# Two modulation panels among the sums of squares, and each down-projection panel split ahead of its tiles

## The reference, cut to what matters

```python
def rms_norm(x, w):
    return x * rsqrt(mean(x * x, axis=-1) + EPS) * w
c_act, cc_act = silu(c), silu(c_ctx)
mod  = split(c_act  @ w_mod[i] + b_mod[i], 6)      # sh1, sc1, g1, sh2, sc2, g2 for x
modc = split(cc_act @ w_mod[i] + b_mod[i], 6)      # the same for ctx
z  = (rms_norm(h,  norm1_w) * (1 + sc1)  + sh1)  @ w_in
zc = (rms_norm(hc, norm1_w) * (1 + csc1) + csh1) @ w_in
a = z[..., :384 + 256 + 32]                        # the "down" part: MLA queries, keys, rope
...                                                # attention mixers, FFN, second layer, second model
```

## Time and profile before

| what | us |
|---|---|
| median of 3 runs | 3116.35 (3114.63 to 3122.04) |
| the profiled execution | 3119.45, its span 3117.7 |
| PE busy in the span | 2812.8 (90%) |
| VectorE, ScalarE, GpSimd busy | 1359.5, 1217.7, 1117.6 |
| granted TensorE clock, mean | 0.951 of full speed |

### The profile page before, as it was taken

How to read it: one execution, slowest core, us unless ns; L and a number is a source line. 1 busy time by engine, 2 the same in 40 slices (tenths; PEclk the granted TensorE clock), 3 DMA queues, 4 the chain that set the end, 5 groups by cost and what they waited for, 6 DMA issues and landing times. The chain is left out here.

```text
span 3117.7 us, 52810 instructions
## 1 busy us (share of the span) xinstructions
PE 2812.8 (90%) x20541; PEld 2502.8 (80%) x20541; DVE 1359.5 (44%) x2405; ACT 1217.7 (39%) x1791; POOL 1117.6 (36%) x457
## 2 busy tenths in 40 slices
PE   6789879799889999888789899899889999988998
PEld 4557667588779999566679799899779989977898
DVE  2443533332343433444434543534564353456433
ACT  2322223333244444422345444444444444444443
POOL 0101020132235565111214455354425555632453
PEclk8899989899989999998999999999999999989999
DMA  5454034533336666211415566465225646622563
GB/s 173 131 180 147 14 83 127 156 91 104 94 109 192 188 194 191 83 29 41 88 48 152 164 197 189 141 198 165 95 82 162 188 138 197 190 84 68 149 186 97
DMA packets 570660, 413.54 MB, mean 133 GB/s; under 512 B 36566, under 2 KB 548252, under 8 KB 570524
## 3 DMA queue, kind: packets, MB, share of 16 engines
q1 hardware_dynamic: 570524, 411.69, 44.6%
HBM read 410.58 MB, written 2.88 MB: 133 GB/s over the span
## 5 line engine op out<-in xcount | busy, mean ns | idle before, releaser
L543 POOL TENSOR_TENSOR wlo<-raw,whi 128x768 fp32r<-128x768 f32 (+2 forms) x353 | 1020.3, 2894 | 1701.6 <-ACT whi L534 1701.2
L566 PE MATMUL psum<-xh_n,whi 128*128 128x256 f32 (+1 forms) x3208 | 932.3, 291 | 79.6 <-DVE rtmp L2612 21.7
L567 PE MATMUL psum<-xl_n,whi 128*128 128x256 f32 (+1 forms) x3208 | 915.1, 285 | 0.0
L568 PE MATMUL psum<-xh_n,wlo 128*128 128x256 f32 (+1 forms) x3208 | 914.7, 285 | 0.0
L543 DVE TENSOR_TENSOR wlo<-raw,whi 128x1280 fp32r<-128x1280 f32 (+2 forms) x353 | 531.2, 1505 | 665.3 <-ACT whi L534 665.1
L534 ACT ACTIVATE whi<-raw 128x2048 fp32r<-128x2048 f32 (+2 forms) x353 | 643.2, 1823 | 396.0 <-PE psum L925 171.8
L566 PEld LDWEIGHTS psum<-xh_n,whi 128*128 128x128 f32 x3208 | 615.4, 192 | 114.4 <-issue 57.7
L568 PEld LDWEIGHTS psum<-xh_n,wlo 128*128 128x128 f32 x3208 | 617.3, 192 | 5.5
L567 PEld LDWEIGHTS psum<-xl_n,whi 128*128 128x128 f32 x3208 | 616.4, 192 | 4.7
L923 PE MATMUL psum<-hidh,whi 128*128 128x256 f32 x1232 | 344.0, 279 | 7.0 <-issue 7.0
L925 PE MATMUL psum<-hidh,wlo 128*128 128x256 f32 x1232 | 343.6, 279 | 0.0
(11 more groups left out here) (337 smaller groups left out, 3804.3 us busy)
## 6 DMA issues: line engine op xcount, KB each, us to landing
raw<-in_ffn_w_in SPq DMA_DIRECT2D x176, 512.0 KB
raw<-in_w_in SPq DMA_DIRECT2D x136, 512.0 KB
raw<-in_w_ffn_in SPq DMA_DIRECT2D x132, 512.0 KB
raw<-in_w_mod SPq DMA_DIRECT2D x96, 512.0 KB
raw<-in_ffn_w_out SPq DMA_DIRECT2D x88, 512.0 KB
raw<-in_w_ffn_out SPq DMA_DIRECT2D x66, 512.0 KB
raw<-in_w_out SPq DMA_DIRECT2D x32, 512.0 KB
raw<-in_w_a_o SPq DMA_DIRECT2D x16, 256.0 KB
```

The costliest lines, as they stand in the source:

```text
L543: eng.tensor_tensor(wlo[slot][:, c0:c1], raw[raw_at[p0] % 3][:, c0:c1], whi[slot][:, c0:c1].bitcast(F32), ALU.subtract).then_inc(sem_, 1)
L566: pe.matmul(dst, sh, mh, start=start and n == 0, stop=False, skip_group_check=True)
L567: pe.matmul(dst, sh, ml, start=False, stop=False, skip_group_check=True)
L568: last = pe.matmul(dst, sl, mh, start=False, stop=n == len(pairs) - 1, skip_group_check=True)
```

## The change

On TensorE the first two modulation panels are taken out of the loop over pairs and put between the sums of squares, and the loop begins with the third panel. On VectorE the copies and vectors of these two panels go ahead of the reciprocal. On ScalarE the high part of down panel 0 goes ahead of the first `xh`, and that of panel j + 1 behind the `xh` tiles of pair j. On VectorE the low part of panel j goes ahead of the pair's `xl`. No arithmetic is added or left out. The line numbers of the changed kernel are 5 to 7 higher at the same instructions.

```diff
-        def pe_sum(pe, tag, nk, bk, cols):
-            for k in range(nk):
+        def pe_sum(pe, tag, nk, bk, cols, ks=None):
+            for k in ks or range(nk):
...
-            pe_sum(pe, ("norm1", 0), 8, 6, slice(0, T))
+            pe.wait_ge(*act_done.at("silu c"))
+            mod_rows(0)
+            pe_sum(pe, ("norm1", 0), 8, 6, slice(0, T), range(0, 2))
+            mod_sum(0)
+            mod_rows(1)
+            pe_sum(pe, ("norm1", 0), 8, 6, slice(0, T), range(2, 4))
+            mod_sum(1)
+            pe_sum(pe, ("norm1", 0), 8, 6, slice(0, T), range(4, 8))
...
-            pe.wait_ge(*act_done.at("silu c"))
-            for j in range(4):
+            pe.wait_ge(*dve_done.at("par"))
+            for j in range(1, 4):
                 mod_rows(2 * j)
-                if j == 1:
-                    pe.wait_ge(*dve_done.at("par"))
-                if j:
-                    open_panel(pe, j - 1)
-                    hi, lo = down_k(2 * j - 2)
-                    for g in range(6):
-                        down_tile(g, 2 * j - 2, hi, lo)
+                open_panel(pe, j - 1)
+                hi, lo = down_k(2 * j - 2)
+                for g in range(6):
+                    down_tile(g, 2 * j - 2, hi, lo)
                 mod_sum(2 * j)
                 mod_rows(2 * j + 1)
...
                 act_squares(act, tg, ...)
+                if l == 0:
+                    split_act(act, 0)
                 for k in range(8):
                     hi_of(k)
-                    if l == 0 and k % 2:
-                        split_act(act, k // 2)
+                    if l == 0 and k in (1, 3, 5):
+                        split_act(act, (k + 1) // 2)
...
-                dve_rstd(dve, tg, slice(0, T))
                 for j in range(4):
                     for m in (2 * j, 2 * j + 1):
                         mod_rows(m)
                         mod_vectors(m)
+                    if j == 0:
+                        dve_rstd(dve, tg, slice(0, T))
                     dve.wait_ge(*dve_done.at(("mod", "vectors", 2 * j + 1)))
                     factors(2 * j, 2 * j + 2)
                     scaled(2 * j)
                     scaled(2 * j + 1)
+                    split_dve(dve, j)
                     lo_of(2 * j)
                     lo_of(2 * j + 1)
-                    split_dve(dve, j)
```

More of the change, by code:

```diff
@@ L801, in down_tile @@
                 return pe.matmul(dst, lo[:, c0:c0 + n], xh[:, k, :], start=False, stop=k == 7, skip_group_check=True)
-            pe.wait_ge(*act_done.at("silu c"))
-            for j in range(4):
+            pe.wait_ge(*dve_done.at("par"))
+            for j in range(1, 4):
                 mod_rows(2 * j)
-                if j == 1:
-                    pe.wait_ge(*dve_done.at("par"))
-                if j:
-                    open_panel(pe, j - 1)
-                    hi, lo = down_k(2 * j - 2)
-                    for g in range(6):
-                        down_tile(g, 2 * j - 2, hi, lo)
+                open_panel(pe, j - 1)
+                hi, lo = down_k(2 * j - 2)
+                for g in range(6):
+                    down_tile(g, 2 * j - 2, hi, lo)
                 mod_sum(2 * j)
                 mod_rows(2 * j + 1)
[L814 to L818, removed]
+                hi, lo = down_k(2 * j - 1)
+                for g in range(6):
+                    m = down_tile(g, 2 * j - 1, hi, lo)
+                m.then_inc(panel_used, 1)
                 mod_sum(2 * j + 1)
```

## The result

Over all runs the changed kernel takes 3102.89 us (median of 16, 3087.58 to 3118.52) against 3117.94 for the one before (16 runs, 3108.44 to 3126.30). The ratio is 0.9948, 95% interval 0.9930 to 0.9967, so it is 15 us faster (10 to 22 by the interval). Forecast were 3103 and 13.2 us. The comparison of the two traces is therefore made at marks in the program and not at the end.

A forecast was written before the change was run, and what follows sets the result against it. TensorE, the busiest engine, was taken to stand still at each down panel for the last low-part piece. Gains 3.39 + 9.84 - 0.2 + 0.2 = 13.2 us off 3116.35 gave 3103; range 3096 to 3109.

The forecast's parts named there:

- a spread of 3: Whole run: scatter of some 3 us from run to run, allowed for in the forecast's own range 3098 to 3107.5.
- The four waits for `wlo`: Down panels: TensorE's first matmul waits for the last piece of the panel's low part, 22.1 us in four waits.
- The panels among the sums: Start: two modulation panels between the sums of squares delay the root 2.12 but start `hn` 3.39 us earlier.
- The split: Chain from `hn` to first down matmul: 3.77 in place of 6.23, 2.46 a turn, 9.84 us in four turns.
- is needed only after 18 matmuls: Down matmuls: the second `xl` tile comes 0.84 after the first, but TensorE needs it only 18 matmuls later.
- The tail: After pair 3: GpSimd's splitting may make VectorE's `kvl` late; 0.2 us lost, ends 0 and 0.8.
- The clock: Behind TensorE's pauses: clock still falls, 3.3 to 6 us of slow work; 0.2 gained, ends -2 and +3.
- is unchanged: Loop: the time from the first down matmul to the next `hn` (42.36 to 55.86) stays as before.
- rival 1: Shortened pauses: clock stays up and the slow stretches go, 7.1 us more gained, 3096; chance 0.08.
- (2): Start: modulation panels late or sum order costs more, first part gives nothing, 9.84 stays, 3106.5; chance 0.06.
- (3): Chain: GpSimd holds VectorE, 1.0 a turn in four turns, 4 us lost, 3107.2; chance 0.09.
- (4): Three turns: ScalarE stopped by a down panel load landing over 14 us after issue; 3127 at 22 us; chance 0.03.

The follow-up runs named there:

- e2: Kernel before with only the high- and low-part split moves, sums of squares in one piece: ratio 0.9951, sums over the latents 11.9 us earlier.
- e3: Changed kernel with VectorE's low part of each down panel put back behind the pair's `xl`: `hn` to matmul 4.60, sums over the latents at 97.94 us.
- the second trace: The changed kernel unaltered, profiled once more on the same chip: sums over the latents at 92.75 us, where its first trace has 93.70.
- e4: Changed kernel with both modulation panels in one piece ahead of the eight sums of squares: root at 31.14, sums over the latents at 97.09 us.
- e9: Changed kernel with TensorE's wait for the second `xl` tile in the MLA stage moved behind the first tile's three matmuls: sums over the latents at 91.51 us.
- e10: Changed kernel with the edits of e5 and e9 together: sums over the latents at 88.44 us, ratio 0.9932 against the kernel before.
- e5: Changed kernel with VectorE's low parts moved out of the chain, panel 0's high part among the squares: `hn` to matmul 2.88, sums over the latents 4.8 us earlier.
- e6: Changed kernel with matmuls of zeros in TensorE's pauses before the down panels: sums over the latents at 87.16 us, 6.5 earlier.
- e8: Changed kernel with GpSimd's low part of down panels 0 and 1 waiting for the first `hn` tile: `hn` to matmul 4.52 in place of 3.58.
- e7: The kernel of e5 with matmuls of zeros in the four pauses: sums over the latents at 84.19 us, 9.5 earlier than in the changed kernel.

## Why the prediction was right, and where a term was off

The time was right, 3103 against 3102.89, and the steps held with these corrections. That it is right to 0.1 is luck: 3103 was counted from the median of three runs, 1.6 under that of all sixteen, and the gain was 15.05 and not 13.2. The runs of the changed kernel also lie 31 us apart, where the range allowed for a spread of 3.

- **What bounds it.** The four waits for `wlo` were the end of the chain; e2 and e3 show that moving the split moves the matmul by as much.
- **The panels among the sums: 3.39 forecast, 3.54 measured.** The step-by-step times were 21.15 for product 1 (21.09), 28.40 for the root (28.21, and 28.75 in the second trace, so `hn` was 3.0 earlier there). Both panels were there in time: neither product waited for a load. I had not seen that the order between the sums also holds the clock (e4).
- **The split: 9.84 forecast, 9.78 measured, but otherwise made up.** The chain is 3.58 and not 3.77 (in the second turn `wlo` starts 1.59 after `hn`, `xl` 0.97 after that and the matmul 1.02 later), so 2.65 a turn in place of 2.46. The fourth chain gave only 1.83. There the step failed by which the second `xl` tile "is needed only after 18 matmuls": in the MLA stage TensorE waits for both tiles ahead of the first matmul. e9 shows it: 4.37 became 3.57, and in e10 3.67 (e5) became 2.88.
- **The tail: 0.2 forecast (0 to 0.8) for VectorE held by GpSimd, nothing seen at the mark.** VectorE's `wlo` of 1280 columns took 1.84 beside GpSimd's (1.49 in the trace of e5), but TensorE came to the latent sums without a wait.
- **The clock: 0.2 forecast, 2.5 measured in the first trace and about 4 in the second.** In the first the clock fell behind all four pauses, as said, but the slow work behind the second and third was 3.3 each where 5.5 and 5.9 had been; in the second it stayed up behind the third. The rows had the first of it: the nearest pauses elsewhere were followed by 3.3. I let a range stand for them instead of taking that row, and this is the mis-sized term. Its sum also left out the slow stretch behind the first pause (4.80 before, 3.10 after). The same error shows in the step by which the time from a first down matmul to the next `hn` "is unchanged": it was 13.50 to 14.00 before and 12.69 to 12.83 in the first trace after, and the turns took 16.3 to 16.4 where 17.3 was forecast.
- **Rivals.** The clock did not stay up throughout (rival 1); e6 shows what that gives, 6.5 in place of 7.1. The panels were in time (2). VectorE is held by GpSimd if they meet (3): e8 measured 0.94 a turn against my 1.0, and in the chains of the change they do not meet. ScalarE waited for the load of a down panel 4 us, but with 9 to spare (4).

The medians are 15.05 apart, and the two traces are 15.64 apart at the mark. Behind it they differ by what is not the change: the same pauses of TensorE stand 15.7 apart at 1781 us, 1.6 at 2231, and the ends of the spans 7.4. No longer wait accounts for it, but the changed kernel's trace has 14 pieces at 118 ns between 1775 and 2150 us, and the one of before has none there.

## What to carry to other kernels

Where a chain ends in several pieces of work, list which need the late operand and which do not: the split of a weight needs only its load, and taking it out of the chain gave three quarters of the gain. When a pause of TensorE is shortened, count the clock behind it as a term, from the pauses of the new length in the same trace, and expect the same pause to bring the clock down in one execution and not in the next. Judge a change of 0.5% at a mark just behind it, since a run may scatter by more than the change is worth.

## What the runs showed of the hardware

- VectorE and GpSimd, both with two inputs from SBUF, hold each other up: VectorE's four `hn` operations took 2.61 in place of 1.67 with a GpSimd piece under way (e8), and such a piece, 1.20 by itself, took 2.07 beside VectorE's `wlo` of 1.06. Beside the reciprocal of one input it took 1.20, and the reciprocal its usual 3.35.
- The same loop of float32 matmuls of 256 columns runs at 113 or at 118 ns each at a granted clock of 1.00, for a whole loop, differently from run to run. In the traces this is a large part of the scatter (18 us between the two of the changed kernel, 23 between e6 and e7). What chooses it was not found.
- In the one trace with both panels ahead of the sums the granted clock was 0.57 in the 3.1 us behind them, with no pause of TensorE over 0.6 us (e4). With the panels between the sums it was 1.00 from 17 to 28 us, in ten traces.
- The same pause does not always bring the clock down: it fell behind nine of eleven pauses of 2.75 or 2.76, and behind none of four of 2.05 or 2.06.
